# Fused two-layer diffusion backbone step: the first output-projection block is loaded and split eight attention steps later

## The reference, cut to what matters

```python
mc = modulation(c_ctx, w_mod, b_mod)      # silu(c) @ w_mod + b_mod, six vectors of 1024
ml = modulation(c, w_mod, b_mod)
u = h @ w_in                              # q1 q2 k1 k2 v, z, x, B, C, dt
# for each query block of 128 tokens and each of 4 heads:
s1 = (q1 * scale) @ k1.T ;  s2 = (q2 * scale) @ k2.T
p = softmax(s1) - lam * softmax(s2) ;  o_a = p @ v
y = bidirectional_ssd(...)
out = concatenate([rms_norm(o_a), rms_norm(y * silu(z))]) @ w_out   # w_out: 1024 x 1024
```

## Time and profile before

| | |
|---|---|
| median of 3 runs | 1546.64 us (1546.28 to 1547.43) |
| the profiled execution | 1545.74 us, of which the span is 1543.9 us |
| PE busy | 1459.8 us, 95% of the span |
| PE weight load, DVE, ACT, POOL busy | 84%, 69%, 35%, 6% |
| granted TensorE clock, mean | 0.982 |
| attention steps 0 to 22 | about 302 to 427 us |

### The profile page before, as it was taken

One profiled execution on the slowest core, in us unless ns is written; L12 is line 12 of the kernel. 1 busy time (PEld: TensorE's weight loads), 2 busy tenths in 40 slices (PEclk: granted clock), 3 DMA queues, 4 the chain that ended last, 5 costly groups with the idle time before them and its releaser, 6 DMA issues.

```text
span 1543.9 us, 23467 instructions
## 1 busy us (share of the span) xinstructions
PE 1459.8 (95%) x9150; PEld 1292.1 (84%) x9150; DVE 1062.4 (69%) x1710; ACT 540.8 (35%) x971; POOL 85.0 (6%) x139
## 2 busy tenths in 40 slices
PE   5899999988999999999999989979999999999995
PEld 3799999755678989998998869758898899889974
DVE  3693455677556877766776785934697677667788
ACT  3333333166425433322332244251642233223310
POOL 1300000010101000000000010000100000000002
PEclk8999999999999999999999999989999999999998
DMA  9611232475652313212321522461132231223141
GB/s 319 197 34 52 80 110 96 137 217 191 231 173 72 123 56 109 82 55 82 109 82 55 204 73 64 149 214 56 55 139 66 83 110 62 75 82 109 55 150 68
DMA packets 130654, 172.78 MB, mean 112 GB/s; under 512 B 3634, under 2 KB 103338, under 8 KB 130562
## 3 DMA queue, kind: packets, MB, share of 16 engines
q1 hardware_dynamic: 123106, 146.57, 29.4%
q0 software_dynamic: 6640, 22.29, 4.4%
q10 hardware_dynamic: 816, 2.65, 0.5%
HBM read 162.58 MB, written 8.91 MB: 111 GB/s over the span
## 4 chain that ended last, share of the span: by engine, by line
PE 81%; DVE 11%; issue 3%; ACT 2%; DMA 2%; POOL 1%; SPq 0%; ACTq 0%; DVEq 0%; POOLq 0%
PE ps L683 37%; PE ps L1169 19%; PE ps L665 7%; PE ps L674 5%; PE ps L716 3%; DVE wlo L1719 2%; PE ps L915 1%; PE ps L1012 1%; DVE p_pad L2429 1%; PE ps L892 1%; PE ps L1035 1%; DMA raw<-in_w_mod_l 1%; PE ps L730 1%; DVE acc L2148 1%; DVE ln_small L2168 1%
## 5 line engine op out<-in xcount | busy, mean ns | idle before, releaser
L1281 ACT ACTIVATE whi<-raw 128x512 fp32r<-128x512 f32 (+2 forms) x189 | 180.9, 967 | 388.3 <-PE ps L683 323.0
L683 PE MATMUL ps<-whi,hid_hi 128*128 128x512 f32 x640 | 250.3, 391 | 5.0 <-DVE wlo L1719 5.0
L683 PE MATMUL ps<-wlo,hid_hi 128*128 128x512 f32 x640 | 249.8, 390 | 0.0
L683 PE MATMUL ps<-whi,hid_lo 128*128 128x512 f32 x640 | 249.6, 390 | 0.0
L1719 DVE TENSOR_TENSOR wlo<-raw,whi 128x512 fp32r<-128x512 f32 (+2 forms) x189 | 208.6, 1113 | 41.0 <-ACT whi L1281 37.4
L683 PE MATMUL ps<-whi,h_hi 128*128 128x256 f32 (+1 forms) x480 | 157.8, 329 | 7.6 <-DVE wlo L1719 6.1
L2141 DVE TENSOR_TENSOR acc<-acc,ps 128x512 f32<-128x512 f32 x120 | 80.3, 684 | 121.8 <-PE ps L683 121.8
L683 PE MATMUL ps<-wlo,h_hi 128*128 128x256 f32 (+1 forms) x480 | 153.7, 320 | 0.0
L683 PE MATMUL ps<-whi,h_lo 128*128 128x256 f32 (+1 forms) x480 | 153.6, 320 | 0.0
L683 PEld LDWEIGHTS ps<-whi,hid_hi 128*128 128x128 f32 x640 | 120.4, 188 | 30.4 <-DVE wlo L1719 5.8
L683 PEld LDWEIGHTS ps<-whi,hid_lo 128*128 128x128 f32 x640 | 120.5, 188 | 25.2
(11 more groups left out here) (305 smaller groups left out, 2802.9 us busy)
## 6 DMA issues: line engine op xcount, KB each, us to landing
raw<-in_w_mod_l SPq DMA_DIRECT2D x44, 1024.0 KB, 5.2
raw<-in_w_up_l SPq DMA_DIRECT2D x32, 1024.0 KB, 5.3
raw<-in_w_down_l SPq DMA_DIRECT2D x32, 1024.0 KB, 5.0
raw<-in_w_in_l SPq DMA_DIRECT2D x12, 1024.0 KB, 5.3
raw<-in_w_out_l SPq DMA_DIRECT2D x8, 1024.0 KB, 5.4
x_spill<-x_tok POOLq DMA_DIRECT2D x10, 512.0 KB, 2.9
x_tok<-x_spill POOLq DMA_DIRECT2D x10, 512.0 KB, 5.9
raw_more<-in_w_in_l SPq DMA_DIRECT2D x4, 1024.0 KB, 11.9
```

Of the source, the lines that this page charges most:

```text
L683: mm = pe.matmul(out, a_of(still, k), w_of(part, k), start=(first and k == 0 and part == 0 and still == 0), stop=(last and k == nk - 1 and ...
L1281: act.activation(ring_piece(whi, w, g), piece(w, g), ACT.Copy).then_inc(hi_done, 1)
```

## The change

Two numbers: the place of the out block in the list, eight mod blocks later, and SKIP from 9 to 17. Nothing is added or removed.

```diff
-    s += [("mod",) + m for m in mods[:11]] + [("out", 0, 1)] + [("mod",) + m for m in mods[11:]]
+    s += [("mod",) + m for m in mods[:19]] + [("out", 0, 1)] + [("mod",) + m for m in mods[19:]]
...
-        SKIP = 9
+        SKIP = 17
```

## The result

| | before | after |
|---|---|---|
| median | 1546.45 us (12 runs, 1544.58 to 1548.44) | 1549.18 us (12 runs, 1548.02 to 1551.58) |
| profiled execution, span | 1545.74, 1543.9 us | 1548.04, 1546.2 us |
| PE busy | 1459.8 us | 1461.9 us |
| scores of step 8 to scores of step 16 | 44.76 us | 40.96 us |
| scores of step 16 to scores of step 19 | 15.48 us | 21.94 us |

The ratio is 1.0017, with an interval of 1.0009 to 1.0025: 0.17% slower, 2.7 us between the medians. The forecast was 1547.9 us, slower by 0.08%. The last row of the table holds the same work in both kernels (the two rows above it don't, one mod block has moved from one to the other), so it is the measure for all that follows; outside it lie 1483.7 us of the span before and 1483.3 after.

What follows compares the result with a forecast made beforehand. PE, busy 95% of the span, was taken to bound the kernel. Waits netting -0.45 us plus 1.7 us for the clock gave +1.25 us on a median of 1546.64, so 1547.9 us, range 1545.3 to 1550.8.

Steps and rivals of the forecast that it cites:

- What goes: Steps 8 to 16: step 8 no longer waits for its load; 3.78 us gained by the scores of step 16.
- The load of m = 34: Before the product of step 16: its load, now right behind the out block, costs a wait of 1.38 us.
- The split's order in step 16: DVE does the gate copy before the low part; the next load is issued 7.43 us after step 16's product starts.
- The load of m = 35: Before step 18's product: lands in 5.2 us, PE idles about 3.5 us; all of the 3.78 but 0.45 given back.
- The clock: Step 18 and head of step 19: half clock behind the second wait costs 1.7 us, bounds 0 and 3.1.
- The full clock: Rival: no costly half clock around step 18, -0.45 us, so 1546.2 us; chance 0.12.
- the covered load: Rival: the wait before step 18's product is hidden, -3.95 us, so 1542.7 us; chance 0.05.
- The late load: Rival: load of m = 35 shares DMA with that of m = 36, takes up to 8.5 us; 1552.6 us; chance 0.11.
- The fourth rival: Rival: new stalls cancel the old, DVE late by step 14's gate copy; about +1.75 us, 1548.4 us; chance 0.07.

Runs made afterwards that it cites:

- split-ahead kernel: Changed kernel with both parts of the split made earlier inside step 16, the low part ahead of the gate copy: 1541.88 us, ratio 0.9962 to before.
- filled kernel: Changed kernel with 3, 3 and 7 matmuls that serve nothing where PE idles in steps 16 to 18: 1547.59 us, ratio 1.0006 to before.
- SKIP 16 with the low part in the gap, again: Second measurement of the changed kernel with SKIP = 16 and DVE's low part in step 16 after the difference: 1542.84 us, ratio 0.9968 to before.
- load alone: Changed kernel, SKIP = 16, low part in step 16, load of m = 36 started only once that of m = 35 landed: 1543.41 us, ratio 0.9973 to before.
- waits filled, too full: Changed kernel with 7, 5 and 14 matmuls that serve nothing where PE idles in steps 16 to 18: 1552.19 us, ratio 1.0027 to before.
- before, wait filled: Kernel before with six matmuls that serve nothing at the end of step 9 on PE: 1546.81 us, ratio 0.9997 to before.
- SKIP 13: Kernel before with the out block moved four mod blocks later instead of eight, and SKIP = 13: 1549.35 us, ratio 1.0009 to before.
- low part in gap: Changed kernel with SKIP = 16 and DVE's low part made in step 16 after the difference, first measurement: 1541.49 us, ratio 0.9959 to before.
- low part before the difference: Changed kernel with SKIP = 16 and DVE's low part made ahead of the difference of step 15: 1542.07 us, ratio 0.9972 to before.
- SKIP 16: Changed kernel with SKIP = 16 instead of 17, the list unchanged: 1543.79 us, ratio 0.9979 to before.
- SKIP 8: Kernel before with SKIP = 8 instead of 9, the list unchanged: 1545.90 us, ratio 0.9997 to before.

## Why the prediction was right, and where it missed

- **What goes: right.** From step 8 to step 16 I had 388.77 - 347.79 = 40.98 us; measured 40.96. DVE's extra gate copy in step 14 cost nothing.
- **The load of m = 34: right in its kind and size.** I had the product of step 16 2.33 us behind that step's scores; it came 2.30 behind (390.16 - 387.86), with 1.81 us of idle time, of which 0.45 would have been there for the gate.
- **The split's order in step 16: right.** High part, then the gate copy, then at once the low part, then the load.
- **The load of m = 35: right.** It took 5.2 us and ended a wait of 3.67 us, forecast 3.5; the exponentials' wait was 1.45, forecast 1.6. The split-ahead kernel shows that it is this wait that gives the gain back: with the load issued early enough it is gone, and the same split delays PE nowhere.
- **The clock: the term that was mis-sized.** I put 1.7 us for one stretch at half clock, behind the second wait. It cost 5.33 us from product to scores instead of 3.85 (409.80 - 404.47), so 1.5. But there was a second one, behind the first wait, which I had not priced at all: I had read from the earlier trace rows that 1.92 us of idle time leave the clock full. It took step 16 from its product to the next scores 6.05 us instead of 4.39, and since the gate copy and the low part stand behind this work, the load of m = 35 was issued 1.65 us later too, 9.08 us behind the product of step 16 (399.24 - 390.16) and not 7.43. The sum of before and after with both: -0.45 + 1.65 + 1.5 = +2.7 us, and 2.66 is measured (62.90 - 60.24). The filled kernel, with both stretches gone, is 2.97 us shorter in these steps. One of the readings that my 1.7 us rested on was off too: the row 1039 to 1040, with 0.55, puts the end of that stretch near 1039.9 and not 1039.1, so the work behind 5.82 us of idle time lost 2.5 us and not 2.1. It moves neither the bounds nor the choice.
- **The rivals.** The full clock and the covered load did not come. The late load did not come here, where the first of the pair landed in 5.2 us; but it is real, if smaller than the 8.5 us that I gave it: 5.9 and 6.9 us in two other kernels. The fourth rival's 1548.4 us is nearer to the measured time than my 1547.9, but by luck: its term, DVE late by the gate copy in step 14, did not come.

The median's +2.7 us agrees with the 2.66 of these steps, which are one execution of each kernel. It is slower, clear of no change, though by less than the 0.2% I had set as the bound. The forecast of +1.25 us had the size at less than half: the chain of waits was right, the first stretch at half clock was missing in it.

## What to carry to other kernels

With two buffers, a transfer that is issued when a slow consumer is done with its buffer has only the work between that moment and its own use to land behind. Before moving such a consumer, count what the main engine still has to do between the release and the use at the new place: here DVE's 6.0 us of idle time ahead of the split were no help, since PE had 3 us of work to cover a load of 5.2. Then look at the order within the step: the out block had landed at 384.2 us (issued at 379.09, 5.1 us) and its high part began at 394.8, because two instructions that wait for PE stood ahead of it.

## What the hardware showed that I had not expected

The length of a wait alone does not tell whether PE's clock falls to 1.2 GHz behind it. The product of step 3 waits for its load in every kernel. Behind 1.90 us (SKIP 16 with the low part in the gap, again), 1.92 (before), 1.94 (load alone), 2.03 (waits filled, too full), 2.08 (before, wait filled), 2.16 (waits filled) and 2.19 (SKIP 13) the granted clock stayed full; behind 2.05 (low part in gap), 2.23 (split ahead) and 2.63 (low part before the difference) it went to half. So it did in the prompt steps behind 1.81 us (changed kernel), 1.85 (split ahead), 2.22 (low part before the difference) and 2.45 (SKIP 16). What else decides it these traces don't show. The stretches lasted some 3.4 us or twice that (SKIP 13, SKIP 8), so each lost about 1.7 or 3.4 us of work, an estimate: half of its length. The wait of step 3 (0.76 to 2.63 us over the executions) and the clock behind it can together differ by more than the whole effect of this change.

Where such a stretch stands ahead of a chain of other engines, its loss is paid once more, by what waits behind: here the load of m = 35, issued 1.65 us later. Where it stands ahead of a load that is late anyway, it is partly free, as in the kernel before, where filling the wait won 0.58 us.
